# First stage of a two-layer hybrid decoder: the shift and scale weights in six pieces, with the accumulator cleared on another engine

## The reference

```python
c_act = silu(c)
for l in range(DEPTH):                       # 2 layers, x is (1, 512, 1024) float32
    mod = c_act @ w_ada[l] + b_ada[l]        # 6 x 1024 values
    shift1, scale1, gate1, shift2, scale2, gate2 = split(mod, 6)
    h = rmsnorm(x, norm_mix_g[l]) * (1 + scale1) + shift1
    x = x + gate1 * mixer(h, w_in[l], w_ret_out[l], w_sb_out[l], w_mix_out[l])
    h2 = rmsnorm(x, norm_mlp_g[l]) * (1 + scale2) + shift2
    x = x + gate2 * (square(relu(h2 @ w_up[l])) @ w_down[l])
return rmsnorm(x, final_g)
```

## Time and profile before

| | |
|---|---|
| median of 3 runs | 2324.07 us (2323.71 to 2324.52) |
| time of the profiled execution | 2324.73 us |
| its span, first to last instruction | 2323.0 us |
| mean granted TensorE clock | 0.999 |
| TensorE, share of the span | 99% |
| first stage, up to the second unit | 49.24 us |

### The profile page before, as it was taken

The page is one execution under the profiler, slowest core; times in us unless marked ns, Lnnn a source line. Parts: engine busy times, 40 slices in busy tenths (PEclk is TensorE's granted clock), DMA queues, the critical chain, the costliest instruction groups (busy, mean ns, idle before and its releaser), DMA issues.

```text
span 2323.0 us, 29667 instructions
## 1 busy us (share of the span) xinstructions
PE 2295.7 (99%) x11946; PEld 1913.9 (82%) x11946; DVE 1047.6 (45%) x1467; ACT 892.9 (38%) x1077; POOL 1126.9 (49%) x1489
## 2 busy tenths in 40 slices
PE   7999999999999999999999999999999999999998
PEld 4888888888878888888898888888888788888887
DVE  5666657545553341122275656441555524221223
ACT  4322233256665242232333322232666834332332
POOL 3454544544444545555544454445444444555552
PEclk9999999999999999999999999999999999999999
DMA  9444534322222323323344443222222222332321
GB/s 299 132 156 142 181 115 145 127 91 73 73 72 73 96 95 99 101 91 100 100 150 131 146 148 129 96 73 92 76 71 72 73 91 91 106 93 91 107 92 55
DMA packets 244152, 252.46 MB, mean 109 GB/s; under 512 B 4016, under 2 KB 241728, under 8 KB 244032
## 3 DMA queue, kind: packets, MB, share of 16 engines
q1 hardware_dynamic: 242496, 247.53, 33.1%
q10 hardware_dynamic: 1536, 3.17, 0.4%
HBM read 248.59 MB, written 2.10 MB: 108 GB/s over the span
## 4 chain that ended last, share of the span: by engine, by line
PE 95%; DVE 3%; ACT 1%; DMA 0%; issue 0%; DVEq 0%; SPq 0%; ACTq 0%
PE proj L870 70%; PE proj L907 12%; PE att L1004 2%; PE proj L892 2%; PE att L1035 2%; PE att L1048 2%; PE att L984 1%; PE att L1058 1%; PE proj L934 1%; DVE att L1285 1%; DVE h_lo L1292 1%; PE att L1013 1%; PE att L934 0%; DMA ya<-in_x 0%; PE proj L952 0%
## 5 line engine op out<-in xcount | busy, mean ns | idle before, releaser
L395 POOL TENSOR_TENSOR w_lo<-w_raw,w_hi 128x256 fp32r<-128x256 f32 x1472 | 1124.8, 796 | 1161.8 <-ACT w_hi L441 1161.2
L870 PE MATMUL proj<-h_hi,w_hi 128*128 128x512 f32 x1568 | 618.7, 395 | 0.3 <-DVE work L1348 0.2
L870 PE MATMUL proj<-h_hi,w_lo 128*128 128x512 f32 x1568 | 611.6, 390 | 0.0
L870 PE MATMUL proj<-h_lo,w_hi 128*128 128x512 f32 x1568 | 611.2, 390 | 0.0
L441 ACT ACTIVATE w_hi<-w_raw 128x1024 fp32r<-128x1024 f32 (+1 forms) x374 | 385.8, 1039 | 523.1 <-PE proj L870 439.1
L870 PEld LDWEIGHTS proj<-h_hi,w_lo 128*128 128x128 f32 x1568 | 294.5, 188 | 62.4
L870 PEld LDWEIGHTS proj<-h_hi,w_hi 128*128 128x128 f32 x1568 | 294.6, 188 | 62.1 <-issue 2.4
L870 PEld LDWEIGHTS proj<-h_lo,w_hi 128*128 128x128 f32 x1568 | 294.9, 188 | 58.9
L870 PE MATMUL proj<-y_lo,w_hi 128*128 128x512 f32 x800 | 311.5, 389 | 0.0
L870 PE MATMUL proj<-y_hi,w_hi 128*128 128x512 f32 x800 | 311.5, 389 | 0.0
L870 PE MATMUL proj<-y_hi,w_lo 128*128 128x512 f32 x800 | 311.5, 389 | 0.0
(11 more groups left out here) (212 smaller groups left out, 2334.6 us busy)
## 6 DMA issues: line engine op xcount, KB each, us to landing
w_raw<-in_w_in SPq DMA_DIRECT2D x88, 1024.0 KB, 5.1
slab<-in_w_ada SPq DMA_DIRECT2D x42, 1024.0 KB, 8.0
w_raw<-in_w_up SPq DMA_DIRECT2D x32, 1024.0 KB, 5.5
w_raw<-in_w_down SPq DMA_DIRECT2D x32, 1024.0 KB, 5.0
w_raw<-in_w_ret_out SPq DMA_DIRECT2D x16, 1024.0 KB, 5.0
w_raw<-in_w_sb_out SPq DMA_DIRECT2D x8, 1024.0 KB, 5.0
w_raw<-in_w_mix_out SPq DMA_DIRECT2D x8, 1024.0 KB, 5.0
first_y<-in_w_ada SPq DMA_DIRECT2D x4, 1024.0 KB, 12.0
```

The lines of the kernel that those rows point to most:

```text
L395: ins = pool.tensor_tensor(w_lo[:, s, ks, :], w_raw[:, s // 2, ks, P * (s % 2):P * (s % 2 + 1)], w_hi[:, s, ks, :], ALU.subtract)
L870: last = pe.matmul(proj[:, j, :], w[:, slot, k, :], a[:, k, :], start=k == 0 and n == 0, stop=k == KT - 1 and n == 2)
```

## The change

- The eight loads of 1 MB in four pairs become six pieces: shift of tiles 0 to 3 (2 MB), scale of 0 and 1, scale of 2 and 3, shift of 4 to 7 (2 MB), scale of 4 and 5, scale of 6 and 7. The total is the same 8 MB. The first unit of `w_in` goes behind the second piece.
- TensorE does the rows of two pieces ahead of the sum of squares, and both turns behind it.
- ScalarE's and VectorE's orders follow the pieces.
- VectorE no longer clears `ya` in this stage. GpSimd does so in one instruction, once x is turned. That instruction stands ahead of the raising of `lo_ready`.

```diff
-FIRST_PAIRS = ADA_FIRST // 2
+FIRST_PIECES = ((0, 0, 4), (1, 0, 2), (1, 2, 2), (0, 4, 4), (1, 4, 2), (1, 6, 2))
@@ SyncE
-            for i in range(FIRST_PAIRS):
-                for part_of in range(2):
-                    col = part_of * D + i * UNIT
-                    sp.dma_start(first_raw[i][:, :, part_of * UNIT:(part_of + 1) * UNIT],
-                                 wada_v[:, 0:1, :, col:col + UNIT].rearrange("p l k n -> p (l k) n")).then_inc(first_in[i], 16)
-                if i == 0:
+            for i, (which, tile, n) in enumerate(FIRST_PIECES):
+                col = which * D + tile * P
+                sp.dma_start(first_raw[i], wada_v[:, 0:1, :, col:col + n * P].rearrange("p l k n -> p (l k) n")
+                             ).then_inc(first_in[i], 16)
+                if i == 1:
                     load(0, 0, win_v[:, 0:1, :, RQ:RQ + UNIT])
             load(0, 1, win_v[:, 0:1, :, RK:RK + UNIT])
@@ GpSimd
             for g in range(LANES):
                 pool.memset(lane_c[LANE * g:LANE * g + 1, :], 1.0).then_inc(consts_made, 1)
+            pool.wait_ge(x_turned, KT)
+            pool.memset(ya[:, :, :], 0.0)
             pool.sem_inc(lo_ready, LO_CREDIT)
@@ ScalarE
-                act.wait_ge(first_taken, k // 2 + 1)
+                act.wait_ge(first_taken, 4 if k >= 4 else 1)
...
                     copy_rows(0)
+                    copy_rows(1)
                     for j in range(2):
                         split_weights(0, 0, j)
                     first_root()
-                    for i in range(1, FIRST_PAIRS):
-                        for k in (2 * i - 2, 2 * i - 1):
-                            first_high(k)
-                        copy_rows(i)
+                    copy_rows(2)
+                    for k in (0, 1):
+                        first_high(k)
+                    copy_rows(3)
+                    for k in (2, 3):
+                        first_high(k)
+                    copy_rows(4)
+                    copy_rows(5)
                     act.dma_start(rope_t, rope).then_inc(rope_in, 16)
-                    for j in range(2):
-                        split_weights(0, 1, j)
-                        first_high(KT - 2 + j)
+                    for k in (4, 5):
+                        first_high(k)
+                    split_weights(0, 1, 0)
+                    for k in (6, 7):
+                        first_high(k)
+                    split_weights(0, 1, 1)
@@ TensorE
             first_rows(0)
+            first_rows(1)
             pe.wait_ge(x_ready, 4)
+            first_mean_square()
             first_turn(0)
-            first_mean_square()
-            for i in range(1, FIRST_PAIRS):
-                first_rows(i)
-                if i < FIRST_PAIRS - 1:
-                    first_products([2 * i - 2])
-                    first_turn(i)
-                    first_products([2 * i - 1])
-                else:
-                    first_turn(i)
-                    first_products([2 * i - 2])
-                    first_products([2 * i - 1])
-            first_products([KT - 2, KT - 1])
+            first_turn(1)
+            first_rows(2)
+            first_turn(2)
+            first_products([0])
+            first_products([1])
+            first_rows(3)
+            first_products([2])
+            first_turn(3)
+            first_rows(4)
+            first_products([3])
+            first_turn(4)
+            first_rows(5)
+            first_turn(5)
+            for ks in ([4], [5], [6, 7]):
+                first_products(ks)
@@ VectorE
-            for i in range(FIRST_PAIRS):
-                take_first(i)
-                ks = (2 * i, 2 * i + 1)
+            take_first(0)
+            take_first(1)
+            for ks in ((0, 1), (2, 3), (4, 5), (6, 7)):
+                if ks[0] == 2:
+                    take_first(2)
+                if ks[0] == 4:
+                    take_first(3)
+                    take_first(4)
                 for k in ks:
                     first_scale(k)
+                if ks[0] == 4:
+                    take_first(5)
                 for k in ks:
                     first_low(k)
-                for k in ks:
-                    dve.memset(ya[:, k, :], 0.0)
```

More of the change, by code:

```diff
@@ L159, in hybrid_trunk @@
         ada_sum = slab[:, 2 * KT * UNIT:(2 * KT + ADA_BATCH) * UNIT].rearrange("p (s n) -> p s n", s=ADA_BATCH)
-        first_raw = (part(0, KT, SEQ), slab[:, 0:KT * SEQ].rearrange("p (k n) -> p k n", k=KT),
-                     first_y[:, 0, :, :], first_y[:, 1, :, :])
+        slab_pair = slab[:, 0:2 * KT * UNIT].rearrange("p (s k n) -> p s k n", s=2, k=KT)
+        y_pair = first_y[:, 1, :, :].rearrange("p a b -> p (a b)").rearrange("p (s k n) -> p s k n", s=2, k=KT)
+        first_raw = (part(0, KT, SEQ), slab_pair[:, 0, :, :], slab_pair[:, 1, :, :],
+                     first_y[:, 0, :, :], y_pair[:, 0, :, :], y_pair[:, 1, :, :])
         x_tok = ya[:, :, :].rearrange("p a b -> p (a b)").rearrange("p (t d) -> p t d", t=TB)
@@ L243, in hybrid_trunk @@
         x_in, out_stored = sem("x_in"), sem("out_stored")
-        first_in = [sem(f"first_in{i}") for i in range(FIRST_PAIRS)]
+        first_in = [sem(f"first_in{i}") for i in range(len(FIRST_PIECES))]
         ada_in = [sem("ada_in0"), sem("ada_in1")]
@@ L462, in copy_rows @@
                 act.wait_ge(rows_done, i + 1)
-                act.activation(row_sum[:, i % 2, :], att[:, 4 + i % 2, :], ACT.Copy).then_inc(rows_copied, 1)
+                cols = P * FIRST_PIECES[i][2]
+                act.activation(row_sum[:, i % 2, 0:cols], att[:, 4 + i % 2, 0:cols], ACT.Copy).then_inc(rows_copied, 1)
             def first_root():
@@ L775, in first_rows @@
             def first_rows(i):
-                pe.wait_ge(first_in[i], 32)
+                pe.wait_ge(first_in[i], 16)
+                cols = P * FIRST_PIECES[i][2]
                 for k in range(KT):
                     g = k % LANES
-                    last = pe.matmul(att[LANE * g:LANE * (g + 1), 4 + i % 2, :], c_lane[:, k, :], first_raw[i][:, k, :],
+                    last = pe.matmul(att[LANE * g:LANE * (g + 1), 4 + i % 2, 0:cols], c_lane[:, k, :], first_raw[i][:, k, :],
                                      start=k < LANES, stop=k >= LANES)
@@ L788, in first_turn @@
                     pe.wait_ge(first_taken, i)
-                for b in range(4):
-                    last = pe.matmul(att[:, 1, 4 * i + b:4 * i + b + 1], row_sum[:, i % 2, P * b:P * (b + 1)],
+                which, tile, n = FIRST_PIECES[i]
+                for b in range(n):
+                    at = KT * which + tile + b
+                    last = pe.matmul(att[:, 1, at:at + 1], row_sum[:, i % 2, P * b:P * (b + 1)],
                                      lane_c[:, :], start=True, stop=True)
@@ L1194, in take_first @@
                 dve.wait_ge(first_turned, i + 1)
[L1195 to L1199, removed]
+                which, tile, n = FIRST_PIECES[i]
+                cols = slice(tile, tile + n)
+                if which == 0:
+                    ins = dve.tensor_tensor(n_shift[:, cols], att[:, 1, cols], mod[:, cols], ALU.add)
+                else:
+                    scale = slice(KT + tile, KT + tile + n)
+                    own.link(dve.scalar_tensor_tensor(mod[:, scale], att[:, 1, scale], 1.0, mod[:, scale], ALU.add, ALU.add))
+                    ins = dve.tensor_tensor(n_scale[:, cols], mod[:, scale], vecs[:, 1, cols], ALU.mult)
+                ins.then_inc(first_taken, 1)
                 dve.wait_ge(first_taken, i + 1)
```

## The result

The changed kernel takes 2328.22 us (median of 17 runs, 2326.65 to 2330.30) against 2323.81 us before (17 runs, 2323.15 to 2324.77). The ratio is 1.0019, with an interval of 1.0012 to 1.0027. So it is slower by 4.4 us. 2325.3 was forecast, with a range of 2321.8 to 2328.0. The kernel before varies by 1.6 us, the changed one by 3.7 us.

The account below looks back on a forecast made before the run. TensorE bounds the kernel: a fixed run of about 2274 us follows the first stage, whose end sets the time. Order 1.0, clears -0.15 and clock 0.35 sum to +1.2 on the median 2324.07: 2325.3, range 2321.8 to 2328.0.

Parts of the forecast that it names:

- Loads: First-stage loads, 3.0 us per MB: first `w_in` unit at 21.7, piece 2 at 24.7, last piece 36.8 as before.
- The raised count: GpSimd's raise comes as the clear is handed over: first `w_in` load issued 16.5, landing 21.6; taken as 0 us.
- Rival A: Raise waits for the clear's end: first unit lands 3.4 us late, together +4.6 to +5.6, about 2329; chance 0.06.
- The clear: GpSimd's clear takes 3.5 us, 16.5 to 20.0, covered; VectorE's dropped clears gain 0.15 us.
- Up to the root, tiles 0 and 1: First stage: root at 23.8, a gain of 0.7 us; tile 0's products at 28.0, both tiles' products taking 3.1.
- Tiles 2 and 3, the last four tiles: Tile 2's products at 35.4, 1.1 us late behind piece 3's rows and copy; VectorE's last step 1.0 late.
- Clock: TensorE's clock may halve in the lull ahead of tile 0's products: 0.7 us at one in two, so 0.35.
- Rival C: Half clock over products of tiles 0 and 1 and piece 3's rows: about +2 us more, 2327.3; chance 0.12.
- a small last piece: Rival: stage ends 9.5 us behind the last landing, at 46.3, or 2321.1 us; chance 0.16 in full or half.

Follow-up runs that it names:

- a1_busy: Changed kernel plus about 3.2 us of unread extra TensorE sums in its waits ahead of tiles 0 and 4: 2324.86 us, against 2324.54 before.
- b1_busy: Kernel before plus eight unread TensorE sums, four behind the rows of pair 0, four behind those of pair 1: 2323.49 us, against 2324.06 before.
- a7_take: Changed kernel with early extra sums, piece 3's rows behind tile 2, and the last piece's copy, turn and take later: 2325.11 us, against 2324.06 before.
- b2_clear: Kernel before with only the clear moved from VectorE to GpSimd, ahead of the raise of the count: 2326.15 us, against 2323.77 before.
- b3_raise: Kernel before with the clear on GpSimd, but the raise ahead of the wait and the clear: 2324.09 us, against 2324.23 before.

## Why the prediction was wrong

The second unit came 3.85 us later than before. The step that failed is the clock: the prediction gave it 0.35 us, it cost 3.7. Point by point, by its own steps:

- *Loads.* Right in the main. Piece 5 landed at 36.4 (20.8 and 15.6 us) where 36.8 was said, and nobody waited for it. The first unit and piece 2 came 1 us earlier than said: ScalarE's wait for the unit ended at 20.71 (21.7 said), TensorE's for piece 2 at 23.72 (24.7 said).
- *The raised count.* Right: the raise ran with the start of the clear, and the first `w_in` load did not hold up the stream. It came at 14.5 and not 16.5, since the transposes began at 9.27 and took 5.18 us in this execution, against 9.72 and 6.67 in the earlier trace rows. Rival A is out: a clear of 3.52 us did not hold the raise. The Trainium skill (Advanced Engine Details and Errata, Sequencer and Instruction Queues) has engine instructions wait for semaphores in their queue while control instructions start. The trace agrees that the raise passes the running clear. The reading that the prediction took from it, that the raise would pass the wait too, is not what happened: the raise came at 14.5, with x turned, and the load with it, not at 6.6.
- *The clear.* Right: 3.52 us, 3.5 said. It ended at 18.03, long before GpSimd's next work at 21.85.
- *Up to the root, tiles 0 and 1.* The root began at 22.62, 23.8 said; the products of tile 0 at 27.31, 28.0 said. Their length is where the sum went wrong.
- *Tiles 2 and 3, the last four tiles.* The mechanism was right: with the clock whole, the products of tile 2 began at 34.40 in the new order (a1_busy) and at 32.92 in the old (b1_busy), and putting the rows of piece 3 behind tile 2 gave 0.95 back. The size was not. The prediction compared with the old kernel as it ran, its fall included, and said 1.0 - 0.15 = 0.85 later. By a1_busy it is 49.35 - 49.24 = 0.11, since the start of the new order came early, products of tile 0 at 27.41 for 28.0. That the two orders lie 1.0 us apart when neither falls is another difference; that it is the predicted figure is luck.
- *Clock.* This is the step that failed, as "I put this at one in two: 0.35". The mechanism was there; the term was mis-sized about tenfold, and even its size in case of a fall, 0.7, was far too small. It measured 2.34 us over tiles 0 and 1 and 1.33 us over the last tiles, 3.7 in all. Two things were missed. The first fall lasted 6.8 us in place of 3.4 and lay over the products of both tiles, from their start at 27.31. And the new order makes further lulls ahead of tile 2 (34.7 to 36.8) and tile 4 (44.3 to 45.5), each over 1 us long, which the working showed and did not price; the second fall came behind the latter.
- Rival C, given 0.12 and +2 us, was the early part of this: 2.34 us, with the products of tiles 0 and 1 at half clock, but the rows of piece 3 at the whole one again. The fall over the last tiles is not in it.

In the prediction's own terms, against the old kernel as it ran, the trace shows 0.11 for the order, where 0.85 was said, and 3.74 for the clock, where 0.35 was said: 3.85 together. From the old order at a whole clock it reads 48.36, + 1.0 for the order, + 3.7 for the clock = 53.1, where the trace has 53.09. The kernel before is 48.36 + 0.9 for its own stretch = 49.24.

What was aimed at is not in this either way: a small last piece can shorten only what follows the last landing, and TensorE was 5.7 us behind it (rows of piece 5 at 42.08, landing at 36.4). In the old order at a whole clock it was not behind at all (b1_busy), so it is the order around the piece that leaves it without effect here.

What stays open: which lull makes the clock fall in a given execution. The three steps among the runs of the changed kernel, 1.4 and 1.9 us apart by their means, at mean clocks of 0.998, 0.997 and 0.996, fit one half-speed stretch of 3.4 us more or less, each worth half its length. That reading is argued from the clocks; only single executions were seen in a trace. The mean is a rough measure, too: it also holds a stretch of half clock at the very end, where TensorE has no work left, and that was 3.2 us long in the changed kernel's trace and 5.1 us in a1_busy's.

## What to carry to other kernels

Where a new order adds waits of TensorE, look first at the granted clock of the work behind each of them, and let the forecast carry that work at half clock as a case of its own. Here it was worth 3.7 us, nearly four times the reordering, and the time also became uneven from run to run. Filling the waits ahead of tile 0 and tile 4 with sums that nobody reads gave 3.7 us back in the trace and 4.1 by the medians; filling one of the two gave 1.0 or 1.7. It does not rule falls out: in a7_take the clock fell with the early sums in.

Compare two orders at the same clock before you say what the order costs: against the old kernel as it ran the new order cost 0.1 us, against the old one without its fall 1.0.

A semaphore raise that is moved behind a wait holds back every load behind it on the queue: ask how many bytes are already queued ahead (2 MB were too few here, 3 MB enough).

## What the runs showed of the hardware

In the changed kernel the mean clock of a whole run told its time: 0.998, 0.997 and 0.996 went with 2326.65 to 2327.01, 2327.99 to 2328.61, and 2329.75 to 2330.30 us. The page TensorE: Matmul & The Clock Gate of the Trainium skill, Part 1, says that a gate sets the clock by how busy the engine has recently been, with two rates. The traces agree on the two rates, 1.00 or 0.50 of 2.4 GHz, and in a1_busy, with sums in two of the lulls, the clock was 1.00 in all windows from 17.2 to 49.9 us.

A raise of a semaphore written behind an instruction without a wait between them is no sign that the instruction is done: L391 ran at 14.5, while the clear ahead of it ended at 18.03.

A GpSimd clear of 128x4096 float32 took 3.52 us, 0.86 ns an element of a partition. VectorE took 0.485 us for 128x512, 0.95 ns an element; the two lengths differ, so the two rates are not compared at equal size.

In b2_clear, with the next load held back until 15.1, the DMA queue moved nothing from 15 to 16 us and 127 GB/s in the microsecond behind, and its last load landed 2.30 us later than in b3_raise.
